# The opening of a hybrid decoder step: norm rows and prompt tokens ahead of the sample, products behind high parts, second weight chunk behind a landing

## What is computed

```python
def rmsnorm(x, w):
    xf = x.astype(jnp.float32)
    y = xf * lax.rsqrt(jnp.mean(xf * xf, axis=-1, keepdims=True) + EPS)
    return (y * w.astype(jnp.float32)).astype(x.dtype)

def retention_layer(x, pos, S0, chunk, norm_w, w_in, gn_w, w_out):
    B, T, _ = x.shape
    h = rmsnorm(x, norm_w) @ w_in            # w_in: 1024 x 6144
    q, k, v, g = jnp.split(h, [qk_w, 2 * qk_w, 2 * qk_w + RET_VW], axis=-1)
    q = rotary(q.reshape(B, T, RET_HEADS, RET_DK), pos)
    ...
```

## Time and profile before

| | |
|---|---|
| median of 3 runs | 524.47 us (524.45 to 525.76) |
| profiled execution | 524.96 us, of which the span of instructions 523.2 us |
| PE busy | 515.1 us, 98% of the span |
| PEld, DVE, ACT, POOL busy | 445.2, 342.4, 257.7, 72.2 us |
| chain that ended last | PE 86%, ACT 5%, DVE 5%, DMA 2%, issue 1% |
| DMA | 125.52 MB, mean 240 GB/s |

### The profile page before, as it was taken

How to read it: one execution, slowest core, us unless ns; L and a number is a source line. 1 busy time by engine, 2 the same in 40 slices (tenths; PEclk the granted TensorE clock), 3 DMA queues, 4 the chain that set the end, 5 groups by cost and what they waited for, 6 DMA issues and landing times.

```text
span 523.2 us, 9484 instructions
## 1 busy us (share of the span) xinstructions
PE 515.1 (98%) x3595; PEld 445.2 (85%) x3595; DVE 342.4 (65%) x628; ACT 257.7 (49%) x511; POOL 72.2 (14%) x81
## 2 busy tenths in 40 slices
PE   7999999999999999999999999999999999999997
PEld 6889977899779977897899999988887778999886
DVE  2775448892878738892698967645756764776531
ACT  5826442572338532562743455744444655555520
POOL 0291004420091004420000130100000000000000
PEclk9999999999999999999999999999999999999999
DMA  7983979999999999989747966516797557682211
GB/s 223 361 303 133 267 243 344 382 297 229 323 352 322 225 262 321 378 264 212 235 147 274 337 195 230 172 52 241 232 337 242 206 187 242 237 299 105 81 50 51
DMA packets 78865, 125.52 MB, mean 240 GB/s; under 512 B 3859, under 2 KB 41828, under 8 KB 78692
## 3 DMA queue, kind: packets, MB, share of 16 engines
q1 hardware_dynamic: 78738, 124.89, 74.1%
q10 hardware_dynamic: 82, 0.02, 0.0%
HBM read 98.93 MB, written 27.57 MB: 242 GB/s over the span
## 4 chain that ended last, share of the span: by engine, by line
PE 86%; ACT 5%; DVE 5%; DMA 2%; issue 1%; ACTq 0%; SPq 0%; DVEq 0%
PE bank L823 37%; PE bank L820 19%; PE bank L809 7%; PE bank L988 3%; PE bank L934 3%; DVE w_lo L1433 2%; PE bank L1002 2%; ACT w_hi L1118 2%; PE bank L1055 1%; PE bank L952 1%; PE bank L906 1%; DMA w_raw<-in_ret_w_in 1%; PE bank L893 1%; PE bank L835 1%; PE bank L1094 1%
## 5 line engine op out<-in xcount | busy, mean ns | idle before, releaser
L1433 DVE TENSOR_TENSOR w_lo<-w_raw,w_hi 128x512 fp32r<-128x512 f32 x206 | 145.1, 742 | 72.1 <-ACT w_hi L1118 71.8
L1118 ACT ACTIVATE w_hi<-w_raw 128x512 fp32r<-128x512 f32 x208 | 118.6, 620 | 49.4 <-PE bank L823 22.2
L823 PE MATMUL bank<-xn_hi,w_hi 128*128 128x320 f32 x320 | 100.6, 318 | 0.9 <-DVE w_lo L1433 0.5
L823 PE MATMUL bank<-xn_hi,w_lo 128*128 128x320 f32 x320 | 97.6, 309 | 0.0
L823 PE MATMUL bank<-xn_lo,w_hi 128*128 128x320 f32 x320 | 97.5, 309 | 0.0
L820 PE MATMUL bank<-w_hi,xn_hi 128*128 128x512 f32 x160 | 65.6, 410 | 0.0
L823 PEld LDWEIGHTS bank<-xn_hi,w_hi 128*128 128x128 f32 x320 | 59.7, 188 | 4.6 <-issue 2.8
L820 PE MATMUL bank<-w_lo,xn_hi 128*128 128x512 f32 x160 | 62.7, 392 | 0.0
L820 PE MATMUL bank<-w_hi,xn_lo 128*128 128x512 f32 x160 | 62.5, 391 | 0.0
L823 PE MATMUL bank<-ym_hi,w_hi 128*128 128x320 f32 x192 | 61.8, 322 | 0.0
L823 PEld LDWEIGHTS bank<-xn_lo,w_hi 128*128 128x128 f32 x320 | 59.8, 188 | 0.5
(11 more groups left out here) (228 smaller groups left out, 743.9 us busy)
## 6 DMA issues: line engine op xcount, KB each, us to landing
w_raw<-in_ret_w_in SPq DMA_DIRECT2D x23, 1024.0 KB, 10.8
st<-in_state_ret SPq DMA_DIRECT2D x32, 512.0 KB, 8.2
out_ret_state_sample<-st SPq DMA_DIRECT2D x32, 512.0 KB, 4.7
w_raw<-in_ret_w_out SPq DMA_DIRECT2D x8, 1024.0 KB, 9.2
w_raw<-in_moba_w_in SPq DMA_DIRECT2D x8, 1024.0 KB, 6.7
cache<-in_cache_k SPq DMA_DIRECT2D x16, 512.0 KB, 5.2
w_raw<-in_w_kv SPq DMA_DIRECT2D x8, 1024.0 KB, 6.1
cache<-in_cache_v SPq DMA_DIRECT2D x16, 512.0 KB, 4.5
```

Of the source, the lines that this page charges most:

```text
L823: mm = pe.matmul(bank[out][:, 0:T], w[:, wk, P * tile:P * tile + P], x[:, k, :], **flags)
L1118: act.activation(w_hi[:, c % 2, part], w_raw[:, c % RAW, part], ACT.Copy).then_inc(w_hi_done, 1)
L1433: dve.tensor_tensor(w_lo[:, c % 2, part], w_raw[:, c % RAW, part], w_hi[:, c % 2, part].bitcast(F32), ALU.subtract).then_inc(w_lo_done, 1)
```

## The change

Five edits, all in the first 30 us of the program.

- **Loads.** SP loads only the identity part of `eye` at first (128x128), the other 132 columns after chunk 1, with a semaphore of their own that step RP and the late user of the mask wait for. SP issues chunk 1 only after the second part of chunk 0 has landed.
- **Norm rows.** PE turns `wrow` after the first token tile, and ACT copies it to `wcols` between its two squares.
- **Prompt tokens.** DVE copies pieces 0 and 1 for the 256 prompt columns as soon as the second prompt tile is turned, and only the 64 sample columns after the sample tile.
- **Products.** In chunk 0 PE waits for the high parts alone ahead of w_hi·x_hi, for `xn_lo` ahead of the second product and for `w_lo` ahead of the third. Three matmuls on zeros stand ahead instead of seven.
- **Order.** The third `w_lo` of chunk 0 goes from POOL to DVE; the `split_hi` and `keep` of ACT stand in another order among the `xn_hi`.

```diff
@@ await_lo
-            if c == 0 and n >= 2:
-                eng.wait_ge(first_lo_done, n - 1)
+            if c == 0 and n == 3:
+                eng.wait_ge(first_lo_done, 1)
             else:
-                eng.wait_ge(w_lo_done, 4 * c + n + 1 - (2 if c else 0))
+                eng.wait_ge(w_lo_done, 4 * c + n + 1 - (1 if c else 0))
@@ load_chunk
-                    await_lo(sp, c - RAW, 1)
+                    await_lo(sp, c - RAW, 2)
@@ block.sync
                 if t == 0:
-                    sp.dma_start(eye[:, :], a["c_eye"]).then_inc(eye_loaded, 16)
+                    sp.dma_start(ident, a["c_eye"][:, 0:P]).then_inc(eye_loaded, 16)
             sp.wait_ge(wrow_loaded, 16 * 5)
             load_chunk(0)
+            sp.wait_ge(second_w_loaded, 16)
             load_chunk(1)
+            sp.dma_start(eye[:, P:2 * P + 4], a["c_eye"][:, P:2 * P + 4]).then_inc(ones_loaded, 16)
@@ project
+                    if c == 0:
+                        pe.wait_ge(w_hi_done, k // 2 + 1)
+                        pe.wait_ge(x_hi_done, k + 1)
...
                     for n, (w, x) in enumerate(((hi, x_hi), (hi, x_lo), (lo, x_hi))):
+                        if c == 0 and n == 1:
+                            pe.wait_ge(x_lo_done, k + 1)
+                        elif c == 0 and n == 2:
+                            await_lo(pe, c, k // 2)
@@ tensor, step X
                         for kt in range(KT):
+                            if t == 1 and kt == 3:
+                                pe.wait_ge(wcols_done, 1)
+                            if t == 2 and kt < 2:
+                                pe.wait_ge(x_copied, kt + 1)
                             mm = pe.transpose(bank[kt][:, c0:c0 + m], st[0:m, t, P * kt:P * kt + P], ident[0:m, 0:m])
-                            if t == 2 and kt == 3:
-                                pe.wait_ge(wrow_loaded, 16 * 5)
-                                mm = pe.transpose(bank[3][:, 384:425], wrow[:, :], ident[0:41, 0:41])
+                            if t == 1 and kt < 2:
+                                mm.then_inc(x_turned, 1)
+                        if t == 0:
+                            pe.wait_ge(wrow_loaded, 16 * 5)
+                            pe.transpose(bank[3][:, 384:425], wrow[:, :], ident[0:41, 0:41]).then_inc(wrow_turned, 1)
-                    for n in range(7):
+                    for n in range(3):
                         mm = pe.matmul(bank[7][:, 384:512], qz[:, 0:P], qz[:, 0:P], start=True, stop=True)
@@ step RP
+                    pe.wait_ge(ones_loaded, 16)
@@ vector, steps X and NORM
+                elif kind == "X":
+                    for kt in range(2):
+                        dve.wait_ge(x_turned, kt + 1)
+                        dve.tensor_copy(xT[:, kt, 0:TP], bank[kt][:, 0:TP]).then_inc(x_copied, 1)
-                        dve.tensor_copy(xT[:, kt, :], bank[kt][:, 0:T]).then_inc(bank_read[kt], 1)
+                        dve.tensor_copy(xT[:, kt, TP:T], bank[kt][:, TP:T]).then_inc(bank_read[kt], 1)
@@ gpsimd
-            for n in range(2, 4):
-                part = slice(CW // 4 * n, CW // 4 * (n + 1))
-                pool.wait_ge(w_hi_done, n + 1)
+            part = slice(3 * CW // 4, CW)
+            pool.wait_ge(w_hi_done, 4)
```

More of the change, by code:

```diff
@@ L424, in build @@
         x_hi_done, x_lo_done = sem("x_hi_done"), sem("x_lo_done")
+        x_turned, x_copied, wrow_turned, ones_loaded = sem("x_turned"), sem("x_copied"), sem("wrow_turned"), sem("ones_loaded")
         rot_done = sem("rot_done")
@@ L794, in project @@
                     x_hi, x_lo = ym_hi, ym_lo
-                first = {"rq": 8, "mq": 16, "mk": 24}.get(kind) if h == 0 and i == 0 else None
+                first = {"mq": 16, "mk": 24}.get(kind) if h == 0 and i == 0 else None
                 stacked = paired and i == 2
@@ L800, in project @@
                     k = base + wk
-                    if i == tile_order(*chunks[c])[0] and paired:
+                    if c == 0:
+                        pe.wait_ge(w_hi_done, k // 2 + 1)
+                        pe.wait_ge(x_hi_done, k + 1)
+                    elif i == tile_order(*chunks[c])[0] and paired:
                         await_lo(pe, c, wk)
@@ L1197, in _ @@
                         done(act.activation(flat[:, D * t:D * t + D], st[:, t, :], ACT.Square, accum_out=rms[:, t:t + 1]))
+                        if t == 0:
+                            act.wait_ge(wrow_turned, 1)
+                            act.activation(wcols[:, 0:41], bank[3][:, 384:425], ACT.Copy).then_inc(wcols_done, 1)
                 elif kind == "NORM":
@@ L1201, in scaled @@
                         if kt < 2:
+                            act.wait_ge(x_copied, kt + 1)
                             await_read(act, kt, "X", kt)
@@ L1212, in keep @@
                         act.activation(xT[:, kt, :], bank[kt][:, 0:T], ACT.Copy).then_inc(bank_read[kt], 1)
-                    await_full(act, 3, "X", 3)
-                    act.activation(wcols[:, 0:41], bank[3][:, 384:425], ACT.Copy).then_inc(wcols_done, 1)
                     act.wait_ge(wcols_done, 1)
@@ L1222, in _ @@
                     scaled(3)
+                    scaled(4)
                     split_hi(0, 2)
-                    scaled(4)
                     scaled(5)
-                    keep(3)
+                    scaled(6)
                     split_hi(0, 3)
-                    scaled(6)
                     scaled(7)
                     keep(2)
+                    keep(3)
                 elif kind == "TILE":
@@ L1475, in _ @@
                         await_full(dve, kt, "X", kt)
-                        dve.tensor_copy(xT[:, kt, :], bank[kt][:, 0:T]).then_inc(bank_read[kt], 1)
+                        dve.tensor_copy(xT[:, kt, TP:T], bank[kt][:, TP:T]).then_inc(bank_read[kt], 1)
+                    dve.wait_ge(x_copied, 2)
                     for kt in range(2):
@@ L1484, in _ @@
                     split_lo(0, 1)
-                    for kt in range(3, KT):
+                    scaled_lo(3)
+                    scaled_lo(4)
+                    split_lo(0, 2)
+                    for kt in range(5, KT):
                         scaled_lo(kt)
@@ L1783, in _ @@
             cos, sin = cst[:, C_COS:C_COS + T], cst[:, C_SIN:C_SIN + T]
-            for n in range(2, 4):
-                part = slice(CW // 4 * n, CW // 4 * (n + 1))
-                pool.wait_ge(w_hi_done, n + 1)
-                pool.tensor_tensor(w_lo[:, 0, part], w_raw[:, 0, part], w_hi[:, 0, part].bitcast(F32), ALU.subtract)\
-                    .then_inc(first_lo_done, 1)
+            part = slice(3 * CW // 4, CW)
+            pool.wait_ge(w_hi_done, 4)
+            pool.tensor_tensor(w_lo[:, 0, part], w_raw[:, 0, part], w_hi[:, 0, part].bitcast(F32), ALU.subtract)\
+                .then_inc(first_lo_done, 1)
             for step in steps:
@@ L1838, in _ @@
                     pool.wait_ge(bias_loaded, 16 * MH)
-                    pool.wait_ge(eye_loaded, 16)
+                    pool.wait_ge(ones_loaded, 16)
                     done.wait()
```

## The result

The changed kernel took 526.35 us (median of 20 runs) against 524.69 us for the kernel before (20 runs beside it): a ratio of 1.0033, 95% interval 1.0024 to 1.0042. It is slower by 0.3%, not faster by 0.3%. The profiled execution took 527.15 us, its span 525.4 us, 2.2 us more than the span of 523.2 us before.

What follows compares the result with a forecast made beforehand. PE was taken to pace the program from step RP, whose start ACT's chain sets; ACT reaching chunk 1 at 15.92 in place of 17.57 gains 1.65 us, so 524.47 - 1.65 = 522.8 us, range 522.3 to 524.4.

Steps and rivals of the forecast that it cites:

- third rival: Opening: chunk 1 keeps 9.2 us from issue to landing, RP at 24.20, a loss of 1.9 us, 526.4 us; chance 0.09.
- RP = S + 4.73: Opening: step RP on PE starts 4.73 us of fixed work after S, ACT's start on chunk 1, predicted at 15.92.
- ACT's start: Opening: ACT's first xn_hi starts at 9.70 us, bounds 9.5 to 9.85, in place of 10.04.
- ACT's 6.22 us on chunk 0: ACT's fourteen operations on chunk 0 take 6.22 us without waits, so ACT starts chunk 1 at 15.92.
- The last part of chunk 0: Its landing moves from 14.24 to 12.4 us, bounds 11.5 to 14.24, ahead of ACT's need at 13.0.
- earlier products bring nothing by themselves: PE's products start at 10.78 against 12.16, but PE then waits 0.85 us at RP, covered by ACT's chain.
- the sentence on chunk 1: Chunk 1, issued at about 10.27, lands between 15.5 and 19.5 us, taken as 15.5 to 15.9, delaying ACT by nothing.
- The load at 28.98: A chunk taken as issued alone at 28.98 us took 5.2 us to land, used for chunk 1's flight.
- There is little idle time between: On the load queue, the last part of chunk 0 still moves when chunk 1 is issued.
- PE has no longer a hole than the ones it had: On PE, fewer matmuls on zeros cost nothing, the granted clock having been 1.00 in the stretches read.
- 1.65 us: The whole gain: RP and all behind it start 1.65 us earlier, carried to the end, 523.31 against the profiled execution.
- the last part's 6.8 us: In the old profile chunk 0's last part took 6.8 us to land, read as held up by loads issued behind it.

Runs made afterwards that it cites:

- e1: The changed kernel without SP's wait for the second part of chunk 0: 524.93 us, ratio to the kernel before 1.0005.
- e7: The changed kernel without SP's wait for the norm rows ahead of chunk 0, the wait for its second part kept: 523.98 us, 0.9980 of the kernel before.
- e2: The kernel before plus only SP's wait for the second part of chunk 0 ahead of chunk 1: 526.40 us, ratio 1.0030.
- e5: The kernel before without SP's wait for the norm rows ahead of chunk 0: 523.92 us, ratio 0.9986.
- e13: The changed kernel again, unaltered, for a further profiled execution: 526.91 us (one execution).
- e8: The changed kernel with SP waiting for all of chunk 0, not its second part, ahead of chunk 1: 525.90 us, 1.0028 of the kernel before.
- e14: e2 again, unaltered, for a second profiled execution: 524.94 us (one execution).
- e16: The changed kernel with SP waiting for only the first part of chunk 0 ahead of chunk 1: 524.79 us, 0.9991 of the kernel before.
- e10: e7 with eight one-column memsets on DVE ahead of its first copies: 523.55 us, 0.9982 of the kernel before.
- e11: The changed kernel again, unaltered, for a second profiled execution: 528.33 us (4 runs), 1.0057 of the kernel before.
- e4: e1 with the whole eye loaded in its old place: 524.50 us, 1.0004 of the kernel before.
- e9: The kernel before with three one-column memsets on DVE ahead of its first copy: 525.17 us, ratio 1.0004.
- e15: e8 again, unaltered, for a second profiled execution: 525.87 us (one execution).

## Why the prediction was wrong, by its own steps

The outcome is its third rival, *the postponed chunk*: that rival had chunk 1 at 19.47, RP at 24.20 and 526.4 us; the runs have 19.04, 23.79 and 526.35. It was given 0.09. Its kind was right, and the closeness of its number is luck. It had chunk 1 issued at 10.27 and 9.2 us in flight, against 11.21 and 7.8, two errors that nearly cancel; and its RP is 0.41 us too late, while the 0.37 us of half clock and the 0.34 us of the stop on DVE are missing from it.

**What held.** RP = S + 4.73 where PE waits for the diagonal: 4.72 in the changed kernel, 4.73 in e1, 4.74 in e7. Where PE comes there last it is longer: 4.89 in e2 and 4.90 in e5, both with the old order of products, and 4.84 in e13, behind the half clock. From RP to the end the shift is carried one for one: RP to `rsb` is 290.74 us before, in e1, e8, e14 and e16, with RP between 21.25 and 22.84. ACT's start: 9.87 for a predicted 9.70, just beyond its bounds. ACT's 6.22 us on chunk 0: 9.96 to 16.06 in e10, 6.10. The last part of chunk 0: 12.4 was 4.96 us from its issue, and it took 4.7 to 5.2 us in the executions with the wait and a late chunk 0, and ACT's idle time ahead of the third split went, or left at most 0.26 us (e11). That earlier products bring nothing by themselves: e1 and e4 are level with the kernel before, with over 1.0 us of waiting at RP. Both also carry the 0.3 us of the stop on DVE, so that level times can hide a gain of that size.

**The step that failed** is the sentence on chunk 1: "I take 15.5 to 15.9, the lower end, because at 10.27 only the last part of chunk 0 is in the queue". It was wrong twice. The issue came at 11.21, not 10.27, because the wait was put at the end of a chain whose first link varies: norm rows landed at 7.7 in this execution and at 6.5 in that of the kernel before. The prediction took the landing of the earlier trace rows as a constant, and named SP's followers but not its leader. And the load took 7.8 us, not 5.2 to 5.6. The load at 28.98 that gave the 5.2 us was not alone, as the earlier trace rows and the prediction call it: a load of 512 KB issued at 21.92 took 8.3 us and was in flight for 1.2 us more. It stands with the six quick executions of the table. Here, at the landing of the second part, the last part had 2.2 us left, and six shares of chunk 1 came late. The prediction wrote "There is little idle time between", but priced that at nothing. It named the interval of 15.5 to 19.5; the likeliest value was taken at the end for which it had one load. In the prediction's own terms, chunk 1's delay of S was put at nothing. It landed at 19.04, 3.1 us behind the latest value of the forecast (15.9): 0.94 us by the later issue and 2.2 us by the longer flight. ACT stood idle for 2.62 us ahead of it, and S was 19.07 in place of 15.92.

**A smaller one.** "PE has no longer a hole than the ones it had", and so a clock that costs nothing, rested on stretches at 1.00 and on the forecast's own case. The delayed chunk made the hole, and the half clock behind it added 0.37 us at RP; in e11, with a hole of 2.49 us, RP to `rsb` took 292.85 us, 2.1 more than before. This belongs to the late chunk's price, and rival (3) left it out.

**The base.** The profiled execution of before had its RP at 22.30; with the same opening e9 had it at 21.64. Some of the 1.65 us was this execution's own lateness. With early chunk 0, e10 came to RP at 20.79 and to 523.42 us, near the predicted 523.31 against the profiled execution; its median is only 1.1 us below that of the kernel before.

**The rule of the Trainium skill.** The prediction weighed the last part's 6.8 us as held up by what is issued behind it. The rows don't bear that out well: without the wait it took 5.4 us in e1, 5.6 in e4 and 5.8 in e9, with it 4.7 to 5.2. Most of the 2.1 us between the two profiles lies in how executions differ. By the Trainium skill (page "DMA: Bandwidth & Descriptors", section "Queues, rings and completion order") each DMA engine consumes its descriptors in ring order, though a later one may finish its write before an earlier one. That a later load can't delay an earlier one was the prediction's own step from there; the remaining 0.2 to 1.1 us neither bear out nor refute it.

## What to carry to other kernels

A wait between two loads turns overlapped latencies into a sum: write down every landing the new wait stands behind, back to the first load, and take each at its late end. Here the first link varied from 6.22 to 8.19 us and the last from 5.1 to 8.4 us in flight. A load that must wait belongs behind something issued early: the same wait cost 0.3% with chunk 0 issued behind the norm rows and showed no cost with it issued at 2.75 us. And before building a gain on a delay that one profiled execution shows, look for it in a second execution with the same queue: the 6.8 us of the last part were 5.8 in e9.

## What the runs showed of the hardware

- Chunk 1, a 1 MB load issued behind others, took 5.1 to 5.2 us with at most 1.3 us of its forerunner left, and 7.4 to 8.4 us with 2.2 us or more left (one execution between, 1.6 us left, 6.7). It isn't a rule for any place: the load at 35.08 in the kernel before took 5.4 us with 2.4 us left. The first of the sixteen landing marks came after 4.2 to 5.0 us in all of them; those of 7.4 us or more differ in five or six late shares. The cause is open.
- The norm rows (20.5 KB in five loads) let SP go on at 6.22 to 8.19 us, over thirteen executions of nine programs that issue them alike. The executions of the program before and its variants have 6.22 to 6.80, those of the changed one and its variants 6.27 to 8.19; why the latter come later isn't known.
- After a hole of 1.88 us on PE, behind 7 us of products without one, the granted clock was 0.50 (1.2 GHz) over 22 to 24 us; e11, with a hole of 2.49 us, had 0.50 over 24 to 28 us and took 1.84 us for RP's six matmuls. e8 with a wait of 1.3 us and e15 with 0.93 us kept 1.00 (2.4 GHz). RP took 1.07 us in both.
- Three one-column memsets at the program's start brought a stop of 0.35 us into DVE's work 400 us later; eight, in the changed opening, took it out.
